# A two-layer transformer block on one core: attention ordered by token tile with the output projection and the next norm woven in, and forget gates taken two banks at a time

## What is computed

```python
def one(qblk):
    s = jnp.einsum('bhqd,bhkd->bhqk', qblk, k).astype(jnp.float32) * scale
    p = jax.nn.softmax(s, axis=-1)
    return jnp.einsum('bhqk,bhkd->bhqd', p.astype(v.dtype), v)
...
y = _branches(u, attn, w_pool[l], pool_scale[l]) @ w_out[l]
x_new = x + gate[:, None, :] * y
```

## Time and profile before

| | |
|---|---|
| three runs | 6090.65, 6092.19, 6095.78 us (median 6092.19) |
| the profiled execution | 6095.19 us |
| its span, first to last instruction | 6093.5 us |
| mean granted TensorE clock | 0.962 |
| TensorE busy (PE) | 5676.1 us, 93% of the span |
| VectorE busy (DVE) | 1210.6 us, 20% |
| ScalarE busy (ACT) | 1088.0 us, 18% |

### The profile page before, as it was taken

One profiled execution on the slowest core, in us unless ns is written; L12 is line 12 of the kernel. 1 busy time (PEld: TensorE's weight loads), 2 busy tenths in 40 slices (PEclk: granted clock), 3 DMA queues, 4 the chain that ended last, 5 costly groups with the idle time before them and its releaser, 6 DMA issues. The chain is left out here.

```text
span 6093.5 us, 55853 instructions
## 1 busy us (share of the span) xinstructions
PE 5676.1 (93%) x22275; PEld 3858.2 (63%) x22275; DVE 1210.6 (20%) x2262; ACT 1088.0 (18%) x1890; POOL 107.8 (2%) x110
## 2 busy tenths in 40 slices
PE   8988889999899999899999499999999999999995
PEld 4444534455444458644666388888888888888884
DVE  3333321244100000120555101010111010111102
ACT  3411102133100000180343010101111111111111
POOL 0000000000000000000000100000000000000001
PEclk9989999999999999899999599999999999999997
DMA  4160002300111111333221145454554545454545
GB/s 176 64 224 0 1 33 92 116 34 34 28 41 34 41 45 38 108 94 111 83 73 46 62 146 157 147 143 160 139 171 134 176 135 168 142 162 144 167 138 188
DMA packets 660687, 638.81 MB, mean 105 GB/s; under 512 B 17363, under 2 KB 595922, under 8 KB 658514
## 3 DMA queue, kind: packets, MB, share of 16 engines
q1 hardware_dynamic: 647888, 593.00, 31.2%
q0 software_dynamic: 8288, 27.29, 1.2%
q10 hardware_dynamic: 4386, 16.82, 0.7%
HBM read 541.62 MB, written 95.45 MB: 105 GB/s over the span
## 5 line engine op out<-in xcount | busy, mean ns | idle before, releaser
L2856 PE MATMUL psum<-arena 128*128 128x272 f32 x7168 | 1647.2, 393 | 7.0 <-issue 7.0
L2856 PEld LDWEIGHTS psum<-arena 128*128 128x128 f32 x7168 | 1362.9, 190 | 289.7 <-issue 8.8
L2871 PE MATMUL psum<-arena 128*128 128x272 f32 x3584 | 831.9, 392 | 0.0
L2871 PEld LDWEIGHTS psum<-arena 128*128 128x128 f32 x3584 | 676.6, 190 | 136.0
L1080 PE MATMUL psum<-arena 128*128 128x512 f32 x1408 | 607.4, 594 | 5.3 <-DMA arena<-in_ffn_w_up 5.3
L1080 PEld LDWEIGHTS psum<-arena 128*128 128x128 f32 x1408 | 268.5, 191 | 343.6 <-issue 343.6
L2789 DVE TENSOR_TENSOR arena<-arena,psum 128x512 f32 x224 | 154.1, 688 | 1504.9 <-ACT arena L2809 1504.9
L1018 PE MATMUL psum<-arena 128*128 128x256 f32 (+1 forms) x1664 | 418.9, 415 | 16.6 <-DMA arena<-in_ffn_w_down 12.5
L1018 PEld LDWEIGHTS psum<-arena 128*128 128x128 f32 x1664 | 318.4, 191 | 116.9 <-issue 75.8
L1296 PE MATMUL psum<-arena 128*128 128x512 f32 (+1 forms) x680 | 297.4, 596 | 2.3 <-PEq L99 2.3
L2809 ACT ACT_TABLE_LOAD x112 | 143.7, 1283 | 863.3 <-PE psum L2856 863.3
(11 more groups left out here) (404 smaller groups left out, 4443.3 us busy)
## 6 DMA issues: line engine op xcount, KB each, us to landing
arena<-in_moe_w_gate SPq DMA_DIRECT2D x112, 1024.0 KB
arena<-in_moe_w_up SPq DMA_DIRECT2D x112, 1024.0 KB
arena<-in_moe_w_down SPq DMA_DIRECT2D x64, 1792.0 KB, 8.3
y_dram<-zeros SPq DMA_DIRECT2D x1, 22528.0 KB, 69.3
arena<-in_c_w_in SPq DMA_DIRECT2D x8, 2048.0 KB, 10.9
y_dram<-arena ACTq DMA_DIRECT2D x8, 2048.0 KB, 6.6
arena<-in_ab_w_in SPq DMA_DIRECT2D x7, 2048.0 KB, 7.9
z_dram<-arena SPq DMA_DIRECT2D x52, 256.0 KB, 2.2
```

The lines of the kernel that those rows point to most:

```text
L2856: last = nc.tensor.matmul(g.ps[:, 2 * f + a, 0:N], wup[b][:, k, a * 256 + f * P:a * 256 + (f + 1) * P], xt[:, k, 0:N], start=(k == 0), sto ...
L2871: last = nc.tensor.matmul(g.ps[:, 4 + b, 0:N], wdn[b][:, k, :], hid[:, k, 0:N], start=(k == 0), stop=(k == EF_T - 1))
```

## The change

**Attention.** One stage takes the place of five (`attention_stage`, `transpose_stage`, `out_proj`, `start_loads`, `norm_stage`). The unit is now a pair of heads of one token tile: 16 pairs p, token tile p // 2, heads 2(p % 2) and 2(p % 2) + 1. The scores of both heads lie end to end in five PSUM banks, once (there is no second set); bank 5 takes the turned probabilities, bank 6 what is woven in, bank 7 the product with the values. In the chunks 0 and 1 the plain products of both heads are issued first, then the two rotated ones, of which one stands on rows 0 to 63 and the other on rows 64 to 127, into different banks. The scores of pair p+1 wait for both exponentials of pair p and are cut in three, with transposes and value products of pair p between them. Into every pair from the third on comes half of the output projection of the token tile before (`project`), and into the pairs the transposes of that tile (`turn_branches`, even pairs) and those of the normed tile two back (`turn_norm`, odd pairs). ScalarE squares and takes the root tile by tile (`norm`), VectorE scales the rows (GpSimd did). The six first normed tiles are stored to `ht_dram` and loaded back when the last scores are made, since their place is that of the queries and keys. The next layer's weights are loaded after the last two halves of the projection.

**Forget gates.** Eight iterations over feature tiles, each on two neighbouring banks (1024 elements a row), in place of sixteen. In iteration f ScalarE makes the first logarithm of tile f and the second of tile f - 1 together, Exp beside Exp and Ln beside Ln. SyncE stores 1024 tokens at a time, 16 stores in all.

```diff
+    R = 2 * NT
+    head_scores = [flat[:, a * KEYS:(a + 1) * KEYS] for a in range(2)]
...
+    for t in range(KEPT):
+        sp.wait_ge(n_taken, 2 * t + 2)
+        sp.dma_start(g.ht_dram[t], made).then_inc(n_st, 16)
+    sp.wait_ge(sc, R)
+    for t in range(KEPT):
+        sp.wait_ge(n_st, 16 * (t + 1))
+        sp.dma_start(ht[:, :, t * P:(t + 1) * P], g.ht_dram[t]).then_inc(ht_in, 16)
     for b in range(2):
+        sp.wait_ge(co_done, 2 * NT - 1 + b)
+        sp.dma_start(wo[b], blocks_of(w_next, 1024 * (b + 1), 512)(0)).then_inc(g.early[b], 16)
+    sp.wait_ge(ht_in, 16 * KEPT)
...
+    def scores(p, i):
+        if i == 0 and p:
+            pe.wait_ge(exped, 2 * p)
+        if i < 2:
+            nope(p, 0, 512 * i, 512)
+            nope(p, 1, 256 + 512 * i, 512)
+            rope(p, 0, 512 * i, 512)
+            rope(p, 1, 256 + 512 * i, 512)
+        else:
+            nope(p, 0, 1024, 256)
+            rope(p, 0, 1024, 256).then_inc(halved, 1)
+            nope(p, 1, 0, 256)
+            pe.wait_ge(halved, p + 1)
+            rope(p, 1, 0, 256).then_inc(sc, 1)
...
+    def project(t, n, half):
+        if half == 0:
+            pe.wait_ge(w_in, 32)
+            pe.wait_ge(bt_taken, 2 * t + 2)
+            if n and t + 1 < NT:
+                pe.wait_ge(co_taken, 2 * t + 1)
+                if t:
+                    pe.wait_ge(n_taken, 2 * t)
+        for k in range(4 * half, 4 * half + 4):
+            last = nc.tensor.matmul(g.ps[:, bank_out(t, n), :], brt[:, k, :], wo[n][:, k, :], start=(k == 0), stop=(k == KD - 1))
+        if half:
+            last.then_inc(co_done, 1)
...
+    for p in range(R):
+        t, odd, more = p // 2, p % 2, p + 1 < R
+        def beside(i):
+            if not odd and t >= 1:
+                turn_branches(t - 1, i)
+            if odd and t >= 2:
+                turn_norm(t - 2, i)
+        def output(half):
+            if t >= 1:
+                project(t - 1, odd, half)
+        turn(p, 0, 0)
+        beside(0)
+        if more:
+            scores(p + 1, 0)
+        turn(p, 0, 1)
+        values(p, 0, 0)
+        beside(1)
+        if more:
+            scores(p + 1, 1)
+        turn(p, 0, 2)
+        values(p, 0, 1)
+        if more:
+            scores(p + 1, 2)
+        values(p, 0, 2)
+        turn(p, 1, 0)
+        output(0)
+        turn(p, 1, 1)
+        values(p, 1, 0)
+        output(1)
+        turn(p, 1, 2)
+        values(p, 1, 1)
+        values(p, 1, 2)
+    last = NT - 1
+    turn_branches(last, 0)
+    turn_branches(last, 1)
+    project(last, 0, 0)
+    project(last, 0, 1)
+    turn_norm(last - 1, 0)
+    turn_norm(last - 1, 1)
+    project(last, 1, 0)
+    project(last, 1, 1)
+    turn_norm(last, 0)
+    turn_norm(last, 1)
...
+    maxima(0)
+    for p in range(R):
+        t, odd = p // 2, p % 2
+        def beside(i):
+            if not odd and t >= 1:
+                take_branches(t - 1, i)
+            if odd and t >= 2:
+                take_norm(t - 2, i)
+        take(p, 0, 0)
+        beside(0)
+        take(p, 0, 1)
+        beside(1)
+        take(p, 0, 2)
+        if p + 1 < R:
+            maxima(p + 1)
+        weighted(p, 0)
+        take(p, 1, 0)
+        if not odd and t >= 2:
+            scaled(t - 2)
+        take(p, 1, 1)
+        take(p, 1, 2)
+        if t >= 1:
+            residual(t - 1, odd)
+        weighted(p, 1)
+    last = NT - 1
+    take_branches(last, 0)
+    take_branches(last, 1)
+    scaled(last - 1)
+    residual(last, 0)
+    take_norm(last - 1, 0)
+    take_norm(last - 1, 1)
+    residual(last, 1)
+    scaled(last)
+    take_norm(last, 0)
+    take_norm(last, 1)
...
+    def exps(p, a):
+        b, u = p % 2, 2 * p + a
+        act.wait_ge(neg, p + 1)
+        if p:
+            act.wait_ge(tr_done, 3 * (u - 2) + 3)
+        if p >= 2:
+            act.wait_ge(o_done, u - 3)
+        nc.scalar.activation(probs[:, a, :], head_scores[a], ACT.Exp, bias=nm[:, b, a:a + 1], scale=scale, accum_out=sm[:, b, a:a + 1]).then_inc(exped, 1)
+    def norm(t):
+        act.wait_ge(xadded, 2 * t + 2)
+        nc.scalar.activation(g.br[:, t, :], g.x[:, t, :], ACT.Square, accum_out=ss[:, t:t + 1])
+        act.drain()
+        nc.scalar.activation(sq[:, t:t + 1], ss[:, t:t + 1], ACT.Sqrt, scale=1.0 / D, bias=g.eps[:, 0:1]).then_inc(root, 1)
+    exps(0, 0)
+    exps(0, 1)
+    for p in range(R):
+        if p % 2 == 0 and p >= 4:
+            norm(p // 2 - 2)
+        if p + 1 < R:
+            exps(p + 1, 0)
+            exps(p + 1, 1)
+    norm(NT - 2)
+    norm(NT - 1)
...
-    start_loads(nc, g, (0, g.w[0], blocks_of(w, 1024, 512)(0)), (1, g.w[1], blocks_of(w, 2048, 512)(0)))
-    norm_stage(nc, g, "n0", g.x, NT, D, g.ht, g.mix_g[:, 0:8])
...
+                if i % 2:
+                    f = i // 2
+                    sp.wait_ge(f_taken, f + 1)
+                    sp.dma_start(g.lk_dram.rearrange(by_chunk)[:, :, f, :], lko.rearrange("p (c t) -> p c t", t=P)).then_inc(k_out, 16)
+                    sp.wait_ge(lf_made, f + 1)
+                    sp.dma_start(g.lf_dram.rearrange(by_chunk)[:, :, f, :], lfo.rearrange("p (c t) -> p c t", t=P)).then_inc(f_out, 16)
...
-                pe.wait_ge(f_taken, i - 7)
+                pe.wait_ge(f_taken, (i - 8) // 2 + 1)
...
+    def forget_a(f):
+        both = g.ps[:, 2 * f % 8:2 * f % 8 + 2, :].rearrange("p a t -> p (a t)")
+        dve.wait_ge(ln1, f + 1)
+        V.scalar_tensor_tensor(y0, both, 0.0, u1, ALU.min, ALU.subtract).then_inc(y_made, 1)
         dve.drain()
         if f:
-            dve.wait_ge(k_out[h], 16 * f)
-        V.scalar_tensor_tensor(lko[h], y0[h], g.ln_1lb[:, f:f + 1], bank, ALU.add, ALU.subtract).then_inc(f_taken, 1)
-    def forget_b(i):
-        f, h = i // 2, i % 2
+            dve.wait_ge(k_out, 16 * f)
+        V.scalar_tensor_tensor(lko, y0, g.ln_1lb[:, f:f + 1], both, ALU.add, ALU.subtract).then_inc(f_taken, 1)
...
+    for f in range(F + 1):
+        if f:
+            forget_b(f - 1)
+        if f < F:
+            forget_a(f)
...
+    for f in range(F + 1):
+        if f < F:
+            act.wait_ge(mm, 2 * f + 2)
+            if f:
+                act.wait_ge(y_made, f)
+            nc.scalar.activation(u1, g.ps[:, 2 * f % 8:2 * f % 8 + 2, :].rearrange("p a t -> p (a t)"), ACT.Abs)
+        if f:
+            act.wait_ge(y_made, f)
+            if f >= 2:
+                act.wait_ge(lf_made, f - 1)
+            nc.scalar.activation(u2, y0, ACT.Abs, bias=cdiff[:, f - 1:f])
         act.drain()
-        nc.scalar.activation(u1[h], u1[h], ACT.Exp, scale=-1.0)
+        if f < F:
+            nc.scalar.activation(u1, u1, ACT.Exp, scale=-1.0)
+        if f:
+            nc.scalar.activation(u2, u2, ACT.Exp, scale=-1.0)
         act.drain()
-        nc.scalar.activation(u1[h], u1[h], ACT.Ln, bias=1.0).then_inc(ln1, 1)
...
+        if f:
+            nc.scalar.activation(u2, u2, ACT.Ln, bias=1.0).then_inc(ln2, 1)
+        if f < F:
+            nc.scalar.activation(u1, u1, ACT.Ln, bias=1.0).then_inc(ln1, 1)
...
-    transpose_stage(nc, g, "brt", g.br, g.brt)
-    out_proj(nc, g, "wout", g.brt, I["w_out"].rearrange("a k n -> (a k) n"), g.gate_row, early=(0, 1))
```

More of the change, by code:

```diff
@@ L881, in transposes, with turn, values @@
+            def turn(p, a, i):
+                u = 2 * p + a
+                k0, k1 = pieces[i]
+                if i == 0:
+                    pe.wait_ge(exped, u + 1)
+                if 3 * u + i:
+                    pe.wait_ge(ev_done, 3 * u + i)
+                for k in range(k0, k1):
+                    last = nc.tensor.transpose(g.ps[:, 5, (k - k0) * P:(k - k0 + 1) * P], probs[:, a, k * P:(k + 1) * P], g.ident)
                 last.then_inc(tr_done, 1)
-            def values(u, i):
-                h, _ = units[u]
-                a, b = pieces[i]
+            def values(p, a, i):
+                h, u = 2 * (p % 2) + a, 2 * p + a
+                k0, k1 = pieces[i]
@@ L896, in _, with turn_branches @@
-            for u in range(N):
-                if u + 1 < N:
-                    scores(u + 1)
-                pe.wait_ge(exped, u + 1)
-                for i in range(3):
-                    transposes(u, i)
-                    if i:
-                        values(u, i - 1)
-                values(u, 2)
+            def turn_branches(t, i):
+                pe.wait_ge(o_done, 4 * (t + 1))
+                if i:
+                    pe.wait_ge(bt_taken, 2 * t + 1)
+                elif t:
+                    pe.wait_ge(co_taken, 2 * t)
+                for k in range(4):
+                    last = nc.tensor.transpose(g.ps[:, bank_turned(t, i), k * P:(k + 1) * P], g.br[:, t, (4 * i + k) * P:(4 * i + k + 1) * P], g.ident)
+                last.then_inc(bt_tr, 1)
@@ new lines, in turn_norm @@
+            def turn_norm(t, i):
+                pe.wait_ge(xs_made, t + 1)
+                if i == 0:
+                    pe.wait_ge(co_taken, min(2 * t + 3, 2 * NT))
+                elif t < KEPT:
```

(31 more changed lines are left out.)

211 lines of the change are left out of this document (70 added, 141 removed).

## The result

The changed kernel takes 5936.8 us (median of 4 executions, 5933.4 to 5939.9) beside 6092.6 us of the kernel before in the same comparison. The ratio is 0.9744, with an interval of 0.9727 to 0.9761. The forecast was 5947.5 us with a range of 5924 to 5988. The gain is 155.7 us, where 145 had been worked out. The execution that was profiled took 5934.6 us, with a span of 5933.0. One execution of the last experiment's kernel took 17441 us in place of 5907; it is left out, and why it took so long is not known.

A forecast was written before the change was run, and what follows sets the result against it. TensorE was taken to bound attention and ScalarE's table loads to delay the forget gates. Attention 365 + 35 + 16 + 4 = 420 saves 121.5 us, forget gates 23: 6095.2 to 5950.7 profiled, 5947.5 median; range 5924 to 5988.

The forecast's parts named there:

- Scores: Attention scores: both rotated products fully side by side, fewer row switches; a pair 8.45 us (now 11.0), sixteen save 40.
- (a): Row pairs in the scores do not fully overlap: 14 us more (5961) or, with none, 27 (5975); chance 0.12.
- four rotated passes "about 1.5 us": Sign of being right, in the score chunks: rows of four passes lasting about 1.5 us, not two times 1.1.
- The work: TensorE's work in the attention stage: pairs 241.6, projection 109.5, transposes of branches and norm 14, together 365 us.
- Cover by the projection: Attention pairs: half a projection covers VectorE's maxima; 0.3 us wait left, 1.2 at even pairs, 10.5 over fourteen pairs.
- Rival (b): Attention cover too thin: 3.8 us waits remain in all fourteen pairs, VectorE's queue late; 43 us more (5990); chance 0.12.
- Clock: Attention: low clock costs 11 us at the start, 5 in pairs 0 and 1, none in steady pairs, 3 at tail.
- Rival (c): Attention's clock stays at 1.2 GHz past pair 1; over all queue work the kernel takes 6297 us; chance 0.02.
- Ends of the stage: Attention: pairs 0 and 1 wait 9.5 and 3.8 us, last pair adds 1.3, final chain idles 10.3, closing 1.
- rival (d): Better in attention: pairs 0 and 1 bring no low clock and the steady waits vanish; 5930 us; chance 0.09.
- Second weight block: Next stage's second block, asked for about 8.8 us before its product: no wait, up to 5 us if slowed.
- Forget gates: Second mixer's projection: TensorE leads in place of ScalarE, no wait remains; 23 us saved, bounds 0 and 25.

The follow-up runs named there:

- the last experiment's kernel: Changed kernel with the branches' transposes behind the next pair's first score chunk and score chunks 1 and 2 as one group: 5906.8 us, ratio 0.9698.
- the two experiments on the row halves: Changed kernel with plain and rotated products alternating (5988.7 us), and, separately, with both heads' rotated products on rows 0 to 63 (6107.6 us, stage 440.3).
- the same-half kernel: Changed kernel with both heads' rotated products on rows 0 to 63: 6107.6 us, inflated by other expert routing; attention stage 440.3 us against 404.0.
- the experiments that take the cover away: Changed kernel with half projections behind each pair's last values, and, separately, with all projections and norms behind the last pair: 6008.7 us each.
- in turns: Changed kernel with score products of chunks 0 and 1 in the old order, plain, rotated, plain, rotated: 5988.7 us, ratio 0.9833.

## Why the prediction was right, point by point

**Scores.** Right. A chunk of two heads takes 2.88 us (forecast 2.97), the third 2.41 (2.52), and the two experiments on the row halves show both terms apart. The 0.09 are in the switches: 2.88 less six passes of 0.43 leaves 0.3 us for the chunk's two, where 0.4 was counted. Of the rivals, (a) is excluded: partial overlap would have left 0.86 us or more per pair, and the same-half kernel shows that the whole 1.71 is saved. The rule of the Trainium skill (TensorE: Matmul & The Clock Gate, Part 3: Packing small matmuls), that matrix instructions start and end in program order and that only different row groups overlap, would have left 14 us there. The kernel issues the first head's product, two passes, ahead of the second's, yet the four passes start two by two (530.818 and 530.824, then 531.351 and 531.358), in pairs 0.53 us apart. The trace does not say which pass belongs to which head. The measurement decides: whatever the order of the program says, none of the four ran alone. One number was written down carelessly: four rotated passes "about 1.5 us" as a sign. The sum had 0.86 for them and 0.2 for the switch, and 1.06 is what came.

**The work.** Right. TensorE was busy 378.2 us in the stage, of which the half clock cost 12.5; 366 are left, where 365 were summed.

**Cover by the projection.** Right in kind. Work in a pair was summed to 22.8 us with the projection and its transposes, and the odd pairs are 22.78. The 0.3 us of wait was not there and the even pairs' 1.2 was 0.85 (23.63 - 22.78, with 0.62 of it shown as a wait). Over fourteen pairs these are 5 us of the difference. Rival (b) did not come; the experiments that take the cover away show what it would have been, and that its price of 43 us left out the clock.

**Clock.** The mechanism was right, the size off: 16 us were counted at the start, and half clock up to the third pair is 16.5 us, of which half, 8 us, is lost. At the tail 8.5 us at half clock cost 4. This is the largest single term of the miss, 8 us at the start and 1 of them back at the tail, of 16 in this stage. Rival (c) found nothing: from +57 to +378 us of the stage no stretch was at half clock.

**Ends of the stage.** Pairs 0 and 1 wait 12.4 us (forecast 13.3). Waits at the end are 7.8 us (2.8 of the last pair's branches, 0.9 and 4.1) where 11.6 were counted, and the stage change is 1.7 us where 1 was. Five us of steady pairs, 7 of clock and 4 here make up the 16 by which the stage is shorter than forecast. The next stage's first product came at 759.0, not 779: 16 us by the stage and 4.4 by the shorter stretch ahead of it. That stretch has no less half clock (21.0 us, 17.1 before) and no less idle time, so why it was shorter is open.

The result lies in the forecast's own range (5935 to 5962), at its lower edge, on the side of rival (d), of whose first condition, no low clock in pairs 0 and 1, half came. The three errors of the stage all have one sign, so the sum did not come out by their cancelling. In the whole, 3 us too much for the forget gates and 1 us elsewhere stand against 16 here and the 4.4 us ahead of the stage, which the forecast does not have: 16 us between the two profiled executions (5950.7 and 5934.6), 11 between the medians, as the changed kernel's profiled execution lies below its median and that of before above.

**Second weight block.** Counted as nothing, up to 5 us. The end of the stage in the changed kernel's timeline:

```profile
742.36 9.19 SPq L892 DMA_DIRECT2D arena<-in_ab_w_in  x2
...
754.47 0.75 DVE L1076 TENSOR_SCALAR arena<-arena,small 128x1024 f32<-128x1024 f32 x1
755.28 1.97 PE L974 MATMUL psum<-ident,arena 128*128 128x128 f32 x8 [4.14 <-DVE arena L1076]
...
758.99 6.20 PE L1466 MATMUL psum<-arena 128*128 128x512 f32 x8 [1.74 <-PEq L99]
```

The block is asked for at 751.17, 7.8 us ahead of the product (8.8 in the forecast), and lands 7.6 us later, at 758.73; the product begins at 758.99, 1.7 us after TensorE's last transpose. It is on the edge. In all eleven other kernels with the new attention stage the same idle time, 1.75 to 2.2 us, ends with that transfer, and the product begins 0.1 to 0.2 us after the landing. By that the next stage starts at most 0.4 us later than here. Nothing was the right value, and it is nothing only by a hair. The 13.6 us of the forecast's upper bound belong to another pair of blocks that the earlier trace rows counts in; before, the second block of this pair took 12.6.

**Forget gates.** The waits of 19.4 us are gone, and 22.8 us came off the projection (forecast 23); no wait is left in it but 2.3 us at its entry. Three were given back behind it (486.4 to 489.4), which the sum did not have. TensorE is idle there as long as before (45.4 us, 45.1 before) but has 83.3 us at half clock where it had 76.0, 3.6 us of lost time. So the forecast's 3 to 4 us for the clock came in the projection and went again in the recurrence, and the mixer as a whole gave 19 to 21 us in all runs with the new forget gates. Why the low clock moved there was not tried. Groups of the changed kernel (count, busy us, mean ns, idle before):

```profile
L2656 ACT ACT_TABLE_LOAD x8 | 10.3, 1283 | 0.4
L2661 ACT ACT_TABLE_LOAD x8 | 10.3, 1283 | 0.4
...
L2648 ACT ACTIVATE arena<-psum 128x1024 f32<-128x1024 f32 x8 | 8.2, 1024 | 51.2 <-PE psum L2342 51.2
```

ScalarE waits 51 us for TensorE: the roles are exchanged, as forecast. Its own part of a tile is 8.8 us (13.73 us from tile to tile, 4.97 of them waiting), where 9 was counted; the forecast's 10.8 with VectorE's 1.2 on the path should have been 10.2 by its own terms, and VectorE was not on the path. By the forecast's steps, from this stage's start at 2424.0, the last logs are done at 2424 + 113 + 18 = 2555; they are at 2553.2, the load back is asked for at 2558.1, and no bank was wanted before it was free. What the forecast did not see is that either half of the edit would have done.

## What to carry to other kernels

Price a wait of TensorE that returns with each iteration at more than its length: here 3.4 us uncovered in each pair cost 2.4 us more through the clock, so filling a gap with work that has to be done anyway paid 1.7 times. Where a kernel alternates between products on 128 and on 64 rows, gather the small ones and put them on opposite halves, down to the last odd chunk: this took 2.5 us from a pair here and another 1.24 when the chunk that shares a bank was done too. And a wait behind an in-order engine's queue was removed here by letting the waiting engine do other work first, and only moved by swapping operations on the releasing one, since its next operation was the one that frees a bank.

## What the runs showed of the hardware

The low clock at the stage's start depends on what runs there. In the kernel before the granted clock was 0.52 for 23 us though TensorE was streaming. Busy time of the first 23 us in the changed kernel:

```profile
355.00:378.00 23.00, 18.12 (x50) 7.68 (x51) 4.44 (x5) 3.93 (x5) 0.00 (x0) 0.79 0.97 365
```

And in the one with the rotated products on the same half:

```profile
359.50:382.50 23.00, 19.48 (x24) 6.67 (x24) 3.06 (x3) 1.55 (x2) 0.00 (x0) 0.50 0.96 365
```

In all ten kernels whose rotated products run side by side the granted clock of these 23 us was 0.72 to 0.79; in the four without (before, its attention with the new forget gates, in turns, same half) it was 0.50 to 0.52, and the low clock ended only 26 to 37 us into the stage. TensorE was not busier for it: 17.7 to 18.1 of 23 us in the ten, 19.5 to 21.7 in the four. The loads beside it took 96 or 97% of the transfer engines in all. The changed kernel and the one on the same half differ in nothing but the rows of the second head's rotated products. So the better clock goes with the two halves being in use together; why it does is open. It made the row pairs worth more than their passes: the kernel in turns has 37 us more at half clock, and its stage is longer by 54 us rather than 40.

Second, a switch between 128 and 64 rows costs 0.15 to 0.2 us, found here in three ways: 0.2 from the steps of the trace of before and from the difference of two experiments (0.78 us for four), 0.15 from the chunk of the changed kernel, whose second switch leads into transposes. The Trainium skill (TensorEngine Tiling (Array Packing), Tiling Modes) says that a change of the tiling mode drains TensorE. The trace agrees in that each such change takes time, and puts that number on it; a drain as such is not to be seen in it.
